# A gated state-space and attention kernel: the drive's second half copied crosswise, link sums on GpSimd, last tiles in token halves

## What is computed

```python
def post_add(x_in, y, i, res_w):
    return x_in + res_w * mod[:, i, 2] * rms_norm_2(y, norm_post[l, i])

x = post_add(x, swiglu(pre(x, 0), ffn_w_in[l, 0], ffn_w_out[l, 0]), 0, FFN_RES)
y = token_mixer(pre(x, 1), ...)
x = post_add(x, y, 1, 1.0)
x = post_add(x, swiglu(pre(x, 2), ffn_w_in[l, 1], ffn_w_out[l, 1]), 2, FFN_RES)
```

## Time and profile before

| | us |
|---|---|
| median of 3 runs | 3424.88 |
| profiled execution | 3428.77 |
| its span, first to last instruction | 3427.0 |
| TensorE busy | 3352.0 (98%) |
| VectorE busy | 1673.1 (49%) |
| ScalarE busy | 1224.2 (36%) |
| GpSimd busy | 435.4 (13%) |
| mean granted TensorE clock | 0.990 |

### The profile page before, as it was taken

One profiled execution on the slowest core, in us unless ns is written; L12 is line 12 of the kernel. 1 busy time (PEld: TensorE's weight loads), 2 busy tenths in 40 slices (PEclk: granted clock), 3 DMA queues, 4 the chain that ended last, 5 costly groups with the idle time before them and its releaser, 6 DMA issues.

```text
span 3427.0 us, 38703 instructions
## 1 busy us (share of the span) xinstructions
PE 3352.0 (98%) x16102; PEld 2640.4 (77%) x16110; DVE 1673.1 (49%) x2190; ACT 1224.2 (36%) x1770; POOL 435.4 (13%) x338
## 2 busy tenths in 40 slices
PE   8999999999999999999999999999999999999998
PEld 6755477788888888888588888878888876888886
DVE  5555666453335635664335534575457533452233
ACT  3374466332223232224533322233223245342222
POOL 0100013122220100112011100110101210210001
PEclk9999999999999999999999999999999999999999
DMA  5412643243333333223032344433431322222221
GB/s 192 148 44 81 185 172 131 109 148 142 140 143 119 107 138 137 75 111 117 21 121 99 135 143 146 135 115 111 152 105 68 124 92 68 86 86 99 99 95 53
DMA packets 78351, 393.40 MB, mean 115 GB/s; under 512 B 8416, under 2 KB 17120, under 8 KB 45024
## 3 DMA queue, kind: packets, MB, share of 16 engines
q1 hardware_dynamic: 66048, 370.41, 30.9%
q10 hardware_dynamic: 12128, 20.52, 1.7%
HBM read 372.02 MB, written 18.87 MB: 114 GB/s over the span
## 4 chain that ended last, share of the span: by engine, by line
PE 91%; DVE 4%; ACT 3%; issue 2%; DMA 0%; ACTq 0%; POOL 0%; SPq 0%; DVEq 0%; POOLq 0%
PE pb L705 22%; PE pb L707 21%; PE pb L706 21%; PE pb L612 3%; PE pb L673 2%; PE pb L674 2%; PE pb L610 2%; PE pb L681 2%; PE pb L876 1%; PE pb L894 1%; PE pb L855 1%; ACT wh L1339 1%; DVE wl L2024 1%; PE pb L1211 1%; PE pb L1161 1%
## 5 line engine op out<-in xcount | busy, mean ns | idle before, releaser
L2024 DVE TENSOR_TENSOR wl<-w,wh 128x2048 fp32r<-128x2048 f32 (+3 forms) x264 | 582.8, 2207 | 889.0 <-ACT wh L1339 886.6
L705 PE MATMUL pb<-XH,wh 128*128 128x512 f32 (+1 forms) x2488 | 985.0, 396 | 2.4 <-DVE wl L2024 1.6
L707 PE MATMUL pb<-XH,wl 128*128 128x512 f32 (+1 forms) x2488 | 970.9, 390 | 0.0
L706 PE MATMUL pb<-XL,wh 128*128 128x512 f32 (+1 forms) x2488 | 970.1, 390 | 0.0
L1339 ACT ACTIVATE wh<-w 128x2048 fp32r<-128x2048 f32 (+3 forms) x264 | 471.7, 1787 | 284.5 <-PE pb L707 188.3
L705 PEld LDWEIGHTS pb<-XH,wh 128*128 128x128 f32 (+1 forms) x2488 | 466.5, 188 | 108.6 <-issue 8.2
L706 PEld LDWEIGHTS pb<-XL,wh 128*128 128x128 f32 (+1 forms) x2488 | 466.5, 187 | 101.7 <-issue 4.6
L707 PEld LDWEIGHTS pb<-XH,wl 128*128 128x128 f32 (+1 forms) x2488 | 465.9, 187 | 100.9
L2998 POOL TENSOR_TENSOR HL<-tmps,HH 128x512 fp32r<-128x512 f32 x120 | 165.6, 1383 | 1312.3 <-ACT HH L1661 1312.3
L705 PE MATMUL pb<-HH,wh 128*128 128x512 f32 x768 | 303.0, 394 | 2.3 <-DVE YT L2780 2.3
L706 PE MATMUL pb<-HL,wh 128*128 128x512 f32 x768 | 301.1, 392 | 0.0
(11 more groups left out here) (479 smaller groups left out, 4057.8 us busy)
## 6 DMA issues: line engine op xcount, KB each, us to landing
w<-in_f_in SPq DMA_DIRECT2D x88, 1024.0 KB, 4.8
mreg<-in_mod_w SPq DMA_DIRECT2D x144, 512.0 KB, 3.6
w<-in_f_out SPq DMA_DIRECT2D x32, 1024.0 KB, 5.0
w<-in_w_up SPq DMA_DIRECT2D x16, 1024.0 KB, 5.7
w<-in_w_dn SPq DMA_DIRECT2D x16, 1024.0 KB, 5.7
w<-in_m_g SPq DMA_DIRECT2D x16, 1024.0 KB, 4.8
w<-in_f_out SPq DMA_DIRECT2D x16, 768.0 KB, 4.2
w<-in_w_rm SPq DMA_DIRECT2D x8, 1024.0 KB, 5.7
```

Source lines behind the costliest of these rows:

```text
L705: mm(dst, hi[:, cs], xh[:, k, :], start=k == 0, stop=False)
L706: mm(dst, hi[:, cs], xl[:, k, :], start=False, stop=False)
L707: x = mm(dst, lo[:, cs], xh[:, k, :], start=False, stop=fin)
L2024: tt(low[:, 0:s.cols], wslots[b % 3][:, 0:s.cols], h[:, 0:s.cols].bitcast(F32), ALU.subtract).then_inc(*DV.up(("lo", b), ("w_free", b)))
```

## The change

Three parts. (1) TensorE multiplies only the first half of the drive. ScalarE copies bank 3 with its two 64-row halves exchanged to `tmps[7]`, in two copies, and VectorE's rotation reads that in place of bank 4. The drive's weights are stored and loaded at half width. (2) In the links the sums of tiles 1 to 7 go from VectorE to GpSimd, and `lo_half` moves from ahead of `scaled(0)` to behind `scaled(3)`. (3) The last four output tiles are computed as eight halves of 256 tokens, first the four of tokens 0 to 255. Sums, root and spread of the first half stand in the middle of the second half's matmuls; half of the remaining sums go to GpSimd, and the output leaves in 16 DMAs.

The core of the diff. First the state space (TensorE, ScalarE, VectorE, and the building of the weights):

```diff
             def drive(l, ft):
...
-                for a in range(2):
-                    for g in range(8):
-                        x = mm(banks[3 + a][:, g * 64:(g + 1) * 64], w[:, a * 1024 + g * 128:a * 1024 + (g + 1) * 128],
-                               U8[:, ft, g * 64:(g + 1) * 64], start=True, stop=True)
+                for g in range(8):
+                    x = mm(banks[3][:, g * 64:(g + 1) * 64], w[:, g * 128:(g + 1) * 128], U8[:, ft, g * 64:(g + 1) * 64],
+                           start=True, stop=True)
                 x.then_inc(*TE.up(("ssm_b", l, ft), ("w_free", b)))
...
+                    elif what == "b":
+                        act.wait_ge(*at("ssm_b", l, ft))
+                        if ft > 0:
+                            act.wait_ge(*at("rotated", l, ft - 1, 1))
+                        for half in range(2):
+                            actf(tmps[7][64 * half:64 * half + 64, :], banks[3][64 - 64 * half:128 - 64 * half, :],
+                                 ACT.Copy).then_inc(*AC.up(("swapped", l, ft)))
...
-                        dve.wait_ge(*at("ssm_b", l, ft))
+                        dve.wait_ge(*at("swapped", l, ft))
                         own()
                         tt(R[0], banks[3][:, :], co, ALU.mult).then_inc(*DV.up())
-                        tt(R[1], banks[4][:, :], si, ALU.mult).then_inc(*DV.up(("rotated", l, ft, 0)))
-                        tt(R[2], banks[4][:, :], co, ALU.mult).then_inc(*DV.up())
+                        tt(R[1], tmps[7][:, :], si, ALU.mult).then_inc(*DV.up(("rotated", l, ft, 0)))
+                        tt(R[2], tmps[7][:, :], co, ALU.mult).then_inc(*DV.up())
                         tt(R[3], banks[3][:, :], si, ALU.mult).then_inc(*DV.up(("rotated", l, ft, 1)))
...
-                        bank = banks[4 + half][:, :].rearrange("p (g h n) -> p g h n", g=4, h=2)
-                        swap = mreg[:, 1024:2048].rearrange("p (g h n) -> p g h n", g=8, h=2)[:, 4 * half:4 * half + 4]
-                        actf(mreg[:, half * 512:half * 512 + 512], banks[4 + half][:, :], ACT.Copy).then_inc(*AC.up())
-                        for h in range(2):
-                            x = actf(swap[:, :, h, :], bank[:, :, 1 - h, :], ACT.Copy)
...
+                        actf(mreg[:, half * 512:half * 512 + 512], banks[4 + half][:, :], ACT.Copy).then_inc(
+                            *AC.up(("w_ev", l, ft, half)))
                     act.wait_ge(*AC.now())
-                    act.dma_start(ssm_in[l, ft], mreg[:, 0:2048]).then_inc(drive_stored, 16)
+                    act.dma_start(ssm_in[l, ft], mreg[:, 0:1024]).then_inc(drive_stored, 16)
```

Then the links (VectorE and GpSimd):

```diff
-                if nxt[1] == 1:
-                    lo_half(st_of[("u", nxt[0])], 1, 1)
                 dve.wait_ge(*at("spread", name))
...
-                added(0)
+                if not final:
+                    dve.wait_ge(*at("y_scaled", r, 0))
+                    tt(hT[:, 0, :], hT[:, 0, :], Y[:, 0, :], ALU.add).then_inc(*DV.up(("h_new", r, 0)))
                 for k in range(8):
                     normed(k)
                     if k < 6:
                         scaled(k + 2)
-                    if k < 7:
-                        added(k + 1)
+                    if k == 1 and nxt[1] == 1:
+                        lo_half(st_of[("u", nxt[0])], 1, 1)
...
+            def h_adds(r):
+
+                for k in range(1, 8):
+                    pool.wait_ge(*at("y_scaled", r, k))
+                    tt(hT[:, k, :], hT[:, k, :], Y[:, k, :], ALU.add).then_inc(*PO.up(("h_new", r, k)))
```

Then the end (TensorE, and VectorE's part behind the waits). `hs(half)` are the half's 256 columns, `last_sums` and `last_spread` are the old sums and spread for one half, and GpSimd's `last_adds` gathers the squares in halves and adds tiles 0, 1, 2, 5, 6, 7 of the first half and 0, 2, 4, 6 of the second:

```diff
+HALF_TILES = [(half, j) for half in range(2) for j in range(4, 8)]
...
+            def half_tiles(s, xh, xl, between):
...
+                for n, (half, j) in enumerate(HALF_TILES):
+                    g, t = j // 2, j % 2
+                    if half == 0 and t == 0:
+                        pe.wait_ge(*at("lo", s.b[g]))
+                    if n < 2:
+                        bank_free(s, s.o[g][t])
+                    else:
+                        pe.wait_ge(*at("ev_half", s.name, *HALF_TILES[n - 2]))
...
+                    for k in range(kts):
+                        cs = slice(k * w + t * 128, k * w + t * 128 + 128)
+                        mm(dst, hi[:, cs], xh[:, k, hs(half)], start=k == 0, stop=False)
+                        mm(dst, hi[:, cs], xl[:, k, hs(half)], start=False, stop=False)
+                        x = mm(dst, lo[:, cs], xh[:, k, hs(half)], start=False, stop=k == kts - 1)
...
+                        if (half, j, k) in between:
+                            between[half, j, k]()
...
                 if r == (1, 2):
-                    last_link(r)
+                    half_tiles(st_of[("out", i, 2)], HH, HL, {(1, 4, 3): lambda: last_sums(r, 0), (1, 5, 1): lambda: last_spread(0)})
+                    last_sums(r, 1)
+                    warm(2)
+                    last_spread(1)
...
+                for more in st_last.ahead[2, 0]:
+                    lo(*more)
+                for j in range(4, 8):
+                    add_y(0, j)
+                own()
+                add_y(1, 4)
+                inverse(0)
+                dve.wait_ge(*at("last_spread", 0))
+                scaled(0, 0, 1, 2)
+                add_y(1, 5)
+                scaled(0, 3, 4)
+                added(0, 3)
+                add_y(1, 6)
+                scaled(0, 5, 6, 7)
+                added(0, 4)
+                add_y(1, 7)
+                inverse(1)
+                dve.wait_ge(*at("last_spread", 1))
+                own()
+                scaled(1, 0, 1)
+                for k in (2, 4, 6):
+                    scaled(1, k)
+                    added(1, k - 1)
+                    scaled(1, k + 1)
+                added(1, 7)
```

More of the change, by code:

```diff
@@ L336, in last_mm, with hs, half_bank @@
             return at("mm", st_of[name].o[-1][-1])
+        def hs(half):
+            return slice(256 * half, 256 * half + 256)
+        def half_bank(s, n):
+            return banks[s.bank[s.o[2][n % 2]]]
         def newc(i, n=8):
@@ L656, in gemm @@
                         continue
+                    if s.halves and g >= 2:
+                        break
                     if s.raw:
@@ L1091, in link, with last_sums, last_spread @@
                 warm(8)
[L1093 to L1099, removed]
+            def last_sums(r, half):
+                pe.wait_ge(*at("y_acc", r, half))
+                for i in (2 * half, 2 * half + 1):
+                    mm(banks[3][:, i:i + 1], tmps[4][:, i * 128:(i + 1) * 128], c("mcol"), start=i == 0, stop=False,
+                       skip_group_check=True)
+                pe.wait_ge(*at("y_sq", r, 7, half))
+                for i in (2 * half, 2 * half + 1):
+                    x = mm(banks[3][:, i:i + 1], tmps[2][:, i * 128:(i + 1) * 128], c("mcol"), start=False, stop=i == 3,
+                           skip_group_check=True)
+                x.then_inc(*TE.up(("last_sums", half)))
+            def last_spread(half):
+                pe.wait_ge(*at("last_inverse", half))
+                for i in (2 * half, 2 * half + 1):
+                    x = mm(banks[4][:, i * 128:(i + 1) * 128], rcol[:, i:i + 1].to_broadcast([128, 128]), c("ident"),
+                           start=True, stop=True)
+                x.then_inc(*TE.up(("last_spread", half)))
             def ffn(l, f):
@@ L1817, in ffn @@
                 if r == (1, 2):
-                    root(("y", r), 512)
+                    for more in st_of[("out", i, 2)].ahead[2, 0]:
+                        hi(*more)
+                    for half, j in HALF_TILES:
+                        last_half(r, j, half)
+                        if (half, j) == (1, 4):
+                            last_root(0)
+                    last_root(1)
                 else:
@@ new lines, in add_y, with inverse @@
+                def add_y(half, j):
+                    dve.wait_ge(*at("mm_half", st_last.name, half, j))
+                    tt(Y[:, j, hs(half)], Y[:, j, hs(half)], half_bank(st_last, j)[:, hs(half)], ALU.add).then_inc(
+                        *DV.up(("ev_half", st_last.name, half, j)))
+                def inverse(half):
+                    cs = slice(2 * half, 2 * half + 2)
+                    dve.wait_ge(*at("last_root", half))
+                    v.reciprocal(rcol[:, cs], rcol[:, cs]).then_inc(*DV.up(("last_inverse", half)))
@@ new lines, in scaled, with added @@
+                def scaled(half, *ks):
+                    for k in ks:
+                        stt(out=Y[:, k, hs(half)], in0=Y[:, k, hs(half)], scalar=gc[:, k:k + 1], in1=banks[4][:, hs(half)],
+                            op0=ALU.mult, op1=ALU.mult).then_inc(*DV.up(("y_scaled", r, k, half)))
+                def added(half, *ks):
+                    for k in ks:
+                        dve.wait_ge(*at("y_scaled", r, k, half))
+                        tt(hT[:, k, hs(half)], hT[:, k, hs(half)], Y[:, k, hs(half)], ALU.add).then_inc(
```

(1 more changed line is left out.)

94 lines of the change are left out of this document (66 added, 28 removed).

## The result

| | before | changed |
|---|---|---|
| median of 14 runs each, us | 3426.19 | 3416.69 |
| lowest to highest, us | 3423.95 to 3432.92 | 3414.40 to 3422.42 |
| ratio, 95% interval | | 0.9970, 0.9962 to 0.9978 |
| profiled execution, its span, us | 3428.8, 3427.0 | 3416.6, 3414.8 |

The change brings 9.5 us by the medians, 10.3 by the ratio (7.5 to 13.0) and 12.2 by the two profiled spans; 11.6 was predicted, 3413.3 on the median. The sum was near. Its first term, the drive, was not: the traces give it the other sign.

The account below looks back on a forecast made before the run. TensorE, with 91% of the span, was taken to bound the kernel. Terms of -2.0 (drive), -6.0 (links) and -3.6 (end) summed to -11.6 us: 3417.2 on the profiled execution, 3413.3 on the median, range 3404 to 3421.

Parts of the forecast that it names:

- the drive: State space, part 1: half the drive's products removed, -4.4 us in two layers, +2.4 for the clock, so -2.0.
- two of the four drives lie ahead of a wait for VectorE: State space: TensorE waits for VectorE's split behind drive 1 and for its last state before the last answer.
- Drives 0 and 3 are followed by VectorE's chain: State space: 1.8 us saved, less 1.2 for ScalarE's copies and 0.4 for a GpSimd collision, leaves 0.2 each.
- The clock: Behind the longer wait after drive 1: a 3.4 us stretch at half rate costs 1.2 us per layer, bounds 0 and 2.4.
- The sums: Links: with tile sums on GpSimd, TensorE no longer waits for the next `XH`; 1.1 us saved per link.
- The second mixer's link: Link ahead of the second mixer: `scaled(0)` starts 1.0 us earlier and the clock may stay up, worth 1.7; -1.8 taken.
- the first mixer's link: Link ahead of the first mixer: 1.1 us saved, `lo_half`'s new place costs 0.2 to 1.5, 0.3 comes back; -0.9.
- half products: The end: 256-column products taken as 0.12 us each from the drive's pace, so 144 make 17.3 us, +1.0.
- the stall for bank and block: The end: the third half tile waits for the second weight block and a bank freed by VectorE's add, 0.9 us.
- last tile to scaling: The end: from last tile to scaling falls from 5.70 to 3.1 us, -2.6, with shorter operations and fewer sums.
- Rival C: The end: 256-column products cost 0.227 us like 512-column ones, making the total +3.8, 3428.7 us; chance 0.06.
- the 109 ns: The end: the skill page's time for a 256-column product, by which 144 would take 15.7 us, a term of -0.6.

Follow-up runs that it names:

- `v_early_low_late`: `v_early`, with GpSimd's `GL` subtractions 1 and 2 also waiting for VectorE's last state: 3395.96 us, ratio 0.9912.
- `warm_gaps`: The changed kernel, with TensorE multiplying constants into an idle bank during both mixer waits: 3410.30 us, ratio 0.9952 to the kernel before.
- `links_alone`: The kernel before with part 2 alone, GpSimd's sums in the links and the moved `lo_half`: 3419.15 us, ratio 0.9978.
- `drive_alone`: The kernel before with part 1 alone, half drive, ScalarE copies and half-width build: 3428.68 us, ratio 1.0008.
- `v_early`: The changed kernel, with the attention's value weights loaded ahead of the drives' and their second block split before drive 0's rotation: 3402.12 us, ratio 0.9932.
- `sums_alone`: The kernel before with GpSimd's sums in the links, `lo_half` left in its old place: 3421.96 us, ratio 0.9988.
- `best`: `v_early_low_late`, with five products of constants ahead of the last answer, into bank 4: 3395.24 us, ratio 0.9908.
- `v_early_full_drive`: `v_early`, with part 1 undone, so the drive is as before the change: 3406.52 us, ratio 0.9946.

## Why the prediction was right, and where it was wrong

**Part 1, -2.0 predicted, +2.7 alone (-0.3 to +5.8), +3.8 in the pair of traces.** The step "two of the four drives lie ahead of a wait for VectorE" held: 0.2 from drive 0, a wait of 4.81 where 4.9 stood, nothing from drive 1, 1.8 from drive 2. Two of its terms failed.

- "Drives 0 and 3 are followed by VectorE's chain, so each brings 1.8 - 1.2 - 0.4 = 0.2 us." At drive 3 the chain is 1.3 us longer from rotation to state, not 0.4: besides the 0.4, the state meets GpSimd's subtraction and takes 1.63, not 0.68. I had costed the collision with the sum, next to the drive, and not followed GpSimd's queue to the next thing in it, which an earlier answer now released into the state. Drive 3 costs 0.7. `v_early_low_late` took the collision away and got the time back.
- The clock, "1.2 per layer (bounds 0 and 2.4)". It cost 3.4: one stretch of 6.8 us, not 3.4, behind the first wait, and the one behind the last answer doubled too. I looked at one wait of two, and took a stretch's length from the only row I had the earlier trace rows. `warm_gaps` measured the whole at 4.8 per mixer against a clock that stays up, which leaves 3.1 more than the 1.7 lost before. The part's upper bound, +0.8, was too low by the traces for this reason.

**Part 2, -6.0 predicted, -7.5 alone (-4.8 to -10.6), -7.2 by clean stretches.** The sums: 1.18 where 1.1 stood. GpSimd kept pace: most of its sums took 1.3 us beside VectorE's operations that read PSUM. The Trainium skill, page "SBUF — State Buffer", section "SBUF: two separate sides", has the port pair that VectorE and GpSimd share as an exclusive lock, which a VectorE operation with two SBUF inputs needs while GpSimd reads SBUF. These traces agree: the sums beside PSUM operations are not lengthened, and the last state is, by 0.95. The second mixer's link: -1.8 predicted, 0.75 and 1.06 measured, where the prediction had 1.0 and the rest from the clock. The mis-sized term is the first mixer's link, -0.9: `lo_half` between scaling and norm was to cost 0.2 to 1.5, and cost nothing, since TensorE had `XH` tiles in hand, and its going from ahead of `scaled(0)` gave 1.06, not 0.3.

**Part 3, -3.6 predicted, -4.3 in two traces (-2.9 to -4.3 over all), -4.8 alone.** Term by term: half products 0.12 apart, as taken from the drive's pace; the stall for bank and block 0.73 (0.9), the wait for the spread 0.67 (0.9); TensorE in all +4.2 (+4.3); last tile to scaling -2.9 (-2.6); scaling -5.5 (-5.3). Rival C is out. So is, for this stream, the 109 ns that the prediction took from the Trainium skill's page "TensorE: Matmul & The Clock Gate", section "Back-to-back issue gap", for such a product: the rows show 0.12 us from start to start.

**The sum.** The three parts alone give +2.7 - 7.5 - 4.8 = -9.6, the medians of both kernels -9.5, their ratio -10.3, the prediction had -11.6. That it came so near is luck in part: part 1's miss of 4.7 was more than half made good by parts 2 and 3, each taken too low (1.5 and 1.2). The two profiled spans differ by 12.2, 2.7 more, and 3.8 of them belong to no part of the change, as the table's last row shows. The runs of `links_alone` alone range over 13.5 us. The prediction's width for the clock, "some 1.7 each, up or down", was needed.

## What to carry to other kernels

Work taken off the bounding engine ahead of a wait for another engine makes the wait longer, and where a longer idle time is followed by a stretch at half clock, as here, the kernel can lose more than it saved: look for each wait behind the edit, and for what the waiting engine's neighbours will now start earlier. If the other engine has idle time ahead of its chain, move the waited-for operation there first; the same half drive cost some 3 us before (by the traces; the runs' interval includes zero), and was worth some 8 to 10 once the split was moved there and a collision taken away. Judge parts of a few us by stretches between fixed points of the trace, when the median moves by chance as much as they do.

## What the runs showed of the hardware

- Idle time of TensorE and the half rate: 4.81 us idle brought 6.8 us at 0.50 in all four mixers of the changed kernel and `drive_alone`; 3.35 did so too, though once in two in `v_early` it brought only 3.4; 1.37 brought 3.4 twice in two (`v_early_low_late`). 1.47 brought 3.4 in some mixers (both of `sums_alone`) and none in others (both of before); there 3.4 came behind the idle times of 0.73 and 0.82 that follow each other at the last answer. With products of constants in the waits there was none in the mixers (`warm_gaps`, `best`). A long idle time is not the only thing that such a stretch follows: in `v_early_full_drive` 6.8 us at 0.50 came once behind an idle time of 0.74 alone.
- Elsewhere half-rate stretches come and go, and the cause stays open. Up to the first mixer's link, which starts at 1457 to 1461 us, TensorE's program is the same in all thirteen kernels, yet between 1450 and 1470 us there were two stretches in five traces, one in four and none in four.
- An operation of VectorE on two SBUF operands takes longer where a GpSimd operation began before it: the state 1.63 in place of 0.68, the second scan 2.22 in place of 1.19.
- A product of 256 columns behind a load of 128x128 takes 0.12 us, about that of 64 columns in the drive and little over half of the 0.227 of 512.
